# Taking the power -1/2 of every norm on VectorE instead of GpSimd in a two-layer hybrid decoder trunk

## The chip, the core and the metric

One core of a Trainium2 chip runs the whole kernel. The metric is the time of one execution in microseconds, from the first to the last work of the core. Engines are named as in the profile: PE is TensorE, DVE is VectorE, ACT is ScalarE, POOL is GpSimd, SP is the SyncE whose queue issues the weight loads.

## The reference

256 tokens of width 1024 pass through two layers. In each layer, with `mod` from a small product of the condition vector with `w_ada`:

```python
h = rms_norm(x) * (1 + sc1) + sh1
proj = h @ w_in[l]                       # q, k, v, qi, ki, wi, cu
q, k = rope(rms_norm(q per head)), rope(rms_norm(k per head))
ki = rope(layer_norm(ki))
attn = attention over the 64 keys that the index scores of qi, ki, wi select
conv = silu(layer_norm(causal depthwise conv, 31 taps, of glu(cu)))
mixed = concat(rms_norm(attn, g1), rms_norm(conv, g2))
x = x + gate1 * (mixed @ w_out[l])
h2 = rms_norm(x) * (1 + sc2) + sh2
x = x + gate2 * peer_ffn(h2)             # 8 heads x 16 experts of 16384 per token
```

Every `rms_norm` and `layer_norm` needs `(mean square or variance + 1e-6) ** -0.5`, one value per token (per token and head for q and k).

## The kernel before

The program is written engine by engine, and each engine runs its instructions in the order written; semaphores tie the engines together. Tokens lie on the 128 partitions in two tiles, `t = 0` and `t = 1`. A layer has two halves.

The first half is projections, convolution, attention and the output projection. VectorE has most of it: the conv taps (`tap`, lines 1074 to 1079), the index key's norm (1151 to 1158), the head norms of q and k (1169 to 1178) with `rotate` (1069 to 1072), the index scores (1102, 1105), the selection of keys (1114, 1116), the layer norm of the convolution (1188 to 1198), its rms norm (1207), and then, interleaved, the logits of six score blocks (`logits(n)`, 1218 to 1220) and `mix(t)`, `add_branch(t)`, `second_norm(t)`. The order at the end is written out by hand:

```python
for n in range(4):
    logits(n)
mix(0)
logits(4)
logits(5)
add_branch(0)
mix(1)
second_norm(0)
add_branch(1)
second_norm(1)
```

One of the four channel groups of the convolution is done by GpSimd: 31 taps, each after the first a TENSOR_SCALAR (line 569) and a TENSOR_TENSOR (line 570). VectorE does one group as a chain in which each tap waits for the one before, and then two groups as a pair (`conv_pair`), alternating, so that a tap need only wait for the one before the last.

PE works through one list of jobs (`plan`); each job takes the next of four PSUM banks in a ring and needs that the job four places earlier has been read out. Weight blocks of 2 MB go through three slots of SBUF (`wring`); SP issues the load of block n when the last job of block n-3 is done. In layer 0 the condition's blocks (`ada`) are worked in between: blocks (0,4) to (0,9) lie between the attention's score blocks. Before `out_tile(0)`, the output projection of the first token tile, PE waits in `use_block` for both halves of `w_out`, then for `mixed_ready` from `mix(0)` on VectorE, then transposes `hb` (line 667, jobs `mT`) and multiplies (line 644).

The second half is the expert part: scores, top 16, and then 256 gathers per token tile of 512 KB each by GpSimd, which VectorE (line 1381) and PE (line 844) consume. Nothing of the change is in it.

The power is taken on GpSimd. VectorE writes the statistic to `rs`, counts up `rsqrt_asked` and waits for `rsqrt_done`; GpSimd's own `rsqrt(width)` waits for the request and runs one TENSOR_TENSOR with the operation pow (line 527). There are nine such calls in a layer: width 2 in `modulated`, for the index key, for the convolution's layer norm and for its rms norm; width 32 for the heads; width 1 in `mix(0)`, `mix(1)`, `second_norm(0)`, `second_norm(1)`. GpSimd's calls stand at fixed places of its order: two of them inside its conv taps, after taps 19 and 24 (`POOL_TAPS`); the one of `mix(0)` stands behind `mod_rows(l, 6, 9)`, a wait for stored condition rows, and behind the issue of the two `modb` transfers.

Of the kernel before, what the change touches and what calls it, by code (L numbers as in the profile page):

```python
# [25 lines left out]
I32 = mybir.dt.int32  # L26
# [5 lines left out]
P = 128  # L32
# [3 lines left out]
NEG = -1.0e30  # L36
TAKEN = -3.0e38
RING = 4
WSLOTS = 3
# [139 lines left out]
def trunk(nc, x, c, positions, w_ada, b_ada, w_in, q_norm_g, k_norm_g, idx_k_ln_g, idx_k_ln_b,  # L179
# [36 lines left out]
    with ExitStack() as ctx:  # L216
        def sb(name, shape, dt=F32):
            return ctx.enter_context(nc.sbuf_tensor(name, shape, dt))

        def sem(name):  # L220
            return ctx.enter_context(nc.semaphore(name))
# [30 lines left out]
        rs = sb("rs", [P, 32])  # L252
        neghalf = sb("neghalf", [P, 32])
        bn6 = sb("bn6", [P, 2, 6])
# [88 lines left out]
        mod2_landed = sem("mod2_landed")  # L343
        rsqrt_asked = sem("rsqrt_asked")
        rsqrt_done = sem("rsqrt_done")
        rope_ready = sem("rope_ready")
# [152 lines left out]
        def _(pool):  # L499
# [9 lines left out]
                                    base=0, pattern=[[-1, P]], channel_multiplier=1))  # L509
            seq_(pool.memset(neghalf[:, :], -0.5))  # L510
            inv_freq = np.power(np.float32(ROPE_THETA), -np.arange(0, ROT, 2, dtype=np.float32) / ROT)
            for i, f in enumerate(inv_freq):
                seq_(pool.memset(invf[:, i:i + 1], float(f)))
            for i, first in enumerate(cand_start):
# [4 lines left out]
                           allow_slow_non_contiguous=True).then_inc(pos_landed, 16)  # L519

            asked = 0

            def rsqrt(width):
                nonlocal asked
                asked += 1
                pool.wait_ge(rsqrt_asked, asked)
                pool.tensor_tensor(rs[:, 0:width], rs[:, 0:width], neghalf[:, 0:width],  # L527
                                   ALU.pow).then_inc(rsqrt_done, 1)

# [9 lines left out]
            for l in range(L):  # L539
# [12 lines left out]
                for i in range(2):  # L552
                    spread(moda[:, i, :], scratch[l, i * D:(i + 1) * D].partition_broadcast(P), mod1_landed)
                rsqrt(2)
                pool.wait_ge(h_ready, 2 * (l + 1))
# [11 lines left out]
                for i in range(1, TAPS):  # L567
                    p = tap_tmp[:, i % 2, 0:T]
                    seq_(pool.tensor_scalar(p, hc[:, ct, i:i + T], cwT[:, ct, i:i + 1], None, ALU.mult))  # L569
                    seq_(pool.tensor_tensor(o, o, p, ALU.add), conv_pool if i == TAPS - 1 else None)  # L570
                    if i == POOL_TAPS[0]:
                        rsqrt(2)
                    if i == POOL_TAPS[1]:
                        rsqrt(32)
                rsqrt(2)
                rsqrt(2)
                mod_rows(l, 4, 5)
# [5 lines left out]
                for i in range(2):  # L583
                    spread(modb[:, i, :], scratch[l, (3 + i) * D:(4 + i) * D].partition_broadcast(P), mod2_landed)
                for t in range(2):
                    rsqrt(1)
                for t in range(2):
                    rsqrt(1)

# [413 lines left out]
        def _(dve):  # L1003
            seq_ = Chain(dve, dve_step)
            asked = [0]

            def rsqrt(last):

                seq_(last, rsqrt_asked, wait=False)
                asked[0] += 1  # L1010
                dve.wait_ge(rsqrt_done, asked[0])

# [32 lines left out]
            def rms_stats(src, t, width, junk=None):  # L1045

                return dve.tensor_tensor_reduce(out=hb[:, t, 0:width] if junk is None else junk, in0=src, in1=src,
                                                scale=1.0 / width, scalar=NORM_EPS, op0=ALU.mult, op1=ALU.add,
                                                accum_out=rs[:, t:t + 1])

            def modulated(l, mod, ready, landed):

                seq_(rms_stats(xs[:, 0, :], 0, D))
                rsqrt(rms_stats(xs[:, 1, :], 1, D))
                dve.wait_ge(landed, 32 * (l + 1))
                seq_(ts(mod[:, 1, :], mod[:, 1, :], 1.0, None, ALU.add))
                for t in range(2):
                    seq_(stt(hb[:, t, :], xs[:, t, :], rs[:, t:t + 1], mod[:, 1, :], ALU.mult, ALU.mult))
                    seq_(tt(hb[:, t, :], hb[:, t, :], mod[:, 0, :], ALU.add), ready)
# [67 lines left out]
            for l in range(L):  # L1127
# [25 lines left out]
                rsqrt(ts(rs[:, 0:2], mv[:, :, 1], NORM_EPS, None, ALU.add))  # L1153
                for t in range(2):
# [12 lines left out]
                for t in range(2):  # L1167
                    sq = hb[:, t, :].rearrange("p (h d) -> p h d", d=DH)
                    seq_(tt(sq, pjh[:, t, 0:16, :], pjh[:, t, 0:16, :], ALU.mult))
                    seq_(dve.tensor_reduce(rs[:, 16 * t:16 * t + 16], sq, AX.X, ALU.add))  # L1170
                rsqrt(ts(rs[:, 0:32], rs[:, 0:32], 1.0 / DH, NORM_EPS, ALU.mult, ALU.add))
                for t in range(2):
# [17 lines left out]
                rsqrt(ts(rs[:, 0:2], mv[:, :, 1], NORM_EPS, None, ALU.add))  # L1190
                dve.wait_ge(out_gains_landed, 64 * (l + 1))
# [7 lines left out]
                for t in range(2):  # L1199
                    dve.wait_ge(silu_done, 2 * l + t + 1)  # L1200
                    ins = rms_stats(hb[:, t, AW:D], t, CW)
                    if t:
                        rsqrt(ins)
                    else:
                        seq_(ins)
# [24 lines left out]
                def mix(t):  # L1230

                    attended(t)
                    rsqrt(dve.tensor_tensor_reduce(out=xtmp[:, 0, :], in0=hb[:, t, 0:AW], in1=hb[:, t, 0:AW],  # L1233
                                                   scale=1.0 / AW, scalar=NORM_EPS, op0=ALU.mult, op1=ALU.add,
                                                   accum_out=rs[:, 0:1]))
                    seq_(stt(hb[:, t, 0:AW], hb[:, t, 0:AW], rs[:, 0:1], out_g[:, 0:AW], ALU.mult, ALU.mult),
                         mixed_ready)
# [12 lines left out]
                def second_norm(t):  # L1250

                    if t == 0:
                        dve.wait_ge(mod2_landed, 32 * (l + 1))
                        seq_(ts(modb[:, 1, :], modb[:, 1, :], 1.0, None, ALU.add))
                    rsqrt(dve.tensor_tensor_reduce(out=hb[:, t, :], in0=xs[:, t, :], in1=xs[:, t, :],
                                                   scale=1.0 / D, scalar=NORM_EPS, op0=ALU.mult, op1=ALU.add,
                                                   accum_out=rs[:, 0:1]))
                    seq_(stt(hb[:, t, :], xs[:, t, :], rs[:, 0:1], modb[:, 1, :], ALU.mult, ALU.mult))
                    seq_(tt(hb[:, t, :], hb[:, t, :], modb[:, 0, :], ALU.add), h2_ready)
# [138 lines left out]

POOL_TAPS = (19, 24)

# [25 lines left out]
```

## Time and profile before

| | |
|---|---|
| median of 3 runs | 2205.45 us (2203.77 to 2205.62) |
| the profiled execution | 2211.21 us, span 2209.4 us |
| PE busy | 923.3 us (42%) |
| DVE busy | 1102.6 us (50%), 2632 instructions |
| ACT busy | 121.1 us (5%) |
| POOL busy | 1129.9 us (51%), 1234 instructions |
| PE clock, mean | 0.682 of full speed |

No engine is busy for more than about half of the span. The core goes through stages with different limits, so each stage has to be read by itself. The busy shares in 40 slices show the two layers: slices 1 to 7 and 21 to 26 (of 55 us each) are the compute stages, and in all others the DMA engines are near fully busy with the gathers.

### The profile page before, as it was taken

To read this page: it belongs to the slowest core of one execution; us is meant where nothing else is said; L and a number is where in the kernel's file an instruction comes from. 1 tells how busy PE (TensorE), PEld (TensorE's weight loads), DVE (VectorE), ACT (ScalarE), POOL (GpSimd) and SP (SyncE) were. 2 spreads that over 40 slices of the span, in tenths; PEclk is the share of its full clock that TensorE was granted. 3 is DMA by queue.
4 is the path that set the end of the run, shared out by engine and by line. 5 is a ranking of instruction groups with operands and counts; after the bars stand their busy time and mean duration, and the time that the engine had idled before them with its cause. 6 is when DMAs were issued, how large, how long until landed. Compare 5 with 4: busy or idle time off the path is not lost. (4 is left out here: it accounts for less than half of the span.)

```text
span 2209.4 us, 16237 instructions
## 1 busy us (share of the span) xinstructions
PE 923.3 (42%) x5604; PEld 462.6 (21%) x5604; DVE 1102.6 (50%) x2632; ACT 121.1 (5%) x255; POOL 1129.9 (51%) x1234
## 2 busy tenths in 40 slices
PE   3985898100145400035449868800014551001554
PEld 2744486100011100001117445700000110000110
DVE  1585316688752078830015852498876206884000
ACT  0122101000000000000001121100000000000000
POOL 1650000566667666666646500046666767666664
PEclk8987898555575755567769968955557685555677
DMA  8336268999999999999973303149999999999997
GB/s 308 120 133 230 88 236 326 409 398 370 351 359 353 356 373 377 368 357 355 368 264 108 127 29 124 39 187 385 367 379 338 350 363 382 368 370 358 373 361 303
DMA packets 208467, 652.32 MB, mean 295 GB/s; under 512 B 20201, under 2 KB 28489, under 8 KB 208385
## 3 DMA queue, kind: packets, MB, share of 16 engines
q0 software_dynamic: 150240, 545.72, 65.7%
q1 hardware_dynamic: 57952, 105.50, 13.2%
q8 instruction: 45, 0.74, 0.1%
q14 instruction: 38, 0.30, 0.0%
q10 hardware_dynamic: 192, 0.05, 0.0%
HBM read 650.11 MB, written 1.10 MB: 295 GB/s over the span
## 5 line engine op out<-in xcount | busy, mean ns | idle before, releaser
L602 POOL DMA_INDIRECT rows<-in_peer_u,u_at x512 | 481.7, 941 | 415.0 <-DVE u_at L1346 174.8
L1381 DVE CUSTOM_DVE_ANT_0 rows<-rows,ps 128x1024 f32<-128x1024 f32 x512 | 603.3, 1219 | 80.3 <-issue 76.6
L610 POOL DMA_INDIRECT rows<-in_peer_v,v_at x512 | 491.7, 960 | 259.8 <-issue 128.6
L844 PE MATMUL ps<-rows,arena 128*32 128x512 f32 x2048 | 385.3, 891 | 345.1 <-DMA rows<-in_peer_v,v_at 299.8
L644 PE MATMUL ps<-arena 128*128 128x256 f32 (+2 forms) x1216 | 355.1, 455 | 10.3 <-ACTq L887 6.2
L667 PE MATMUL ps<-ident,coef 128*128 128x128 f32 x4 | 1.9, 476 | 747.5 <-DVE coef L1387 377.3
L644 PEld LDWEIGHTS ps<-arena 128*128 128x128 f32 x1216 | 233.3, 197 | 127.9 <-issue 92.6
L844 PEld LDWEIGHTS ps<-rows,arena 128*32 128x32 f32 x2048 | 80.0, 140 | 645.2 <-issue 643.9
L1364 DVE TENSOR_TENSOR bias<-ps,arena 128x512 f32<-128x512 f32 x8 | 5.5, 690 | 356.2 <-PE ps L844 356.1
L667 PEld LDWEIGHTS ps<-ident,coef 128*128 128x128 f32 x4 | 0.7, 182 | 748.6 <-DVE coef L1387 377.8
L527 POOL TENSOR_TENSOR rs<-rs,neghalf 128x2 f32<-128x2 f32 (+2 forms) x18 | 21.1, 1175 | 213.3 <-DVE rs L1233 73.8
L1349 DVE CAST v_at<-ps 128x128 uint32<-128x128 f32 x4 | 1.2, 291 | 240.9 <-remote 240.5
L1079 DVE SCALAR_TENSOR_TENSOR arena<-arena,cwT 128x256 f32<-128x256 f32 x180 | 90.0, 550 | 2.4
L667 PE MATMUL ps<-ident,arena 128*128 128x128 f32 (+1 forms) x252 | 48.7, 354 | 89.3 <-ACTq L953 25.3
L884 ACT COPY arena<-ps 128x512 f32<-128x512 f32 (+2 forms) x110 | 62.5, 569 | 357.4 <-PE ps L644 214.4
L659 PE MATMUL ps<-arena,cact 128*32 128x128 f32 x1536 | 62.8, 330 | 45.7 <-DMA brows<-in_b_ada 32.7
L1274 DVE MAX8 arena<-arena 128x8 f32<-128x128 f32 x64 | 15.6, 286 | 132.7 <-ACTq L887 116.6
L659 PEld LDWEIGHTS ps<-arena,cact 128*32 128x32 f32 x1536 | 53.3, 134 | 53.8 <-issue 27.9
L569 POOL TENSOR_SCALAR arena<-arena,cwT 128x256 f32<-128x256 f32 x60 | 61.0, 1017 | 5.5
L537 POOL DMA_DIRECT2D arena<-mod_rows x12 | 6.7, 567 | 107.6 <-DMA mod_rows<-stages 104.7
L667 PEld LDWEIGHTS ps<-ident,arena 128*128 128x128 f32 (+1 forms) x252 | 38.9, 186 | 100.4 <-issue 30.5
L997 ACT ACTIVATE dots<-dots 128x128 f32<-128x128 f32 x4 | 1.2, 309 | 995.0 <-remote 796.0
(161 smaller groups left out, 723.7 us busy)
## 6 DMA issues: line engine op xcount, KB each, us to landing
arena<-in_w_ada SPq DMA_DIRECT2D x24, 2048.0 KB
arena<-in_w_in SPq DMA_DIRECT2D x8, 2048.0 KB
arena<-in_peer_wq SPq DMA_DIRECT2D x8, 2048.0 KB
arena<-in_w_in SPq DMA_DIRECT2D x8, 1024.0 KB
arena<-in_w_out SPq DMA_DIRECT2D x4, 2048.0 KB
rows<-in_peer_u,u_at POOLq DMA_INDIRECT x512
rows<-in_peer_v,v_at POOLq DMA_INDIRECT x512
arena<-mod_rows POOLq DMA_DIRECT2D x12, 512.0 KB, 5.5
```

What stands on the lines that cost most here:

```text
L527: pool.tensor_tensor(rs[:, 0:width], rs[:, 0:width], neghalf[:, 0:width], ALU.pow).then_inc(rsqrt_done, 1)
L569: seq_(pool.tensor_scalar(p, hc[:, ct, i:i + T], cwT[:, ct, i:i + 1], None, ALU.mult))
L602: pool.indirect_dma_start(row(n), None, u_rows, bass.IndirectOffsetOnAxis(ap=u_at[:, t, k:k + 1], axis=0)).then_inc(row_landed[n % SLOTS], 16)
L610: pool.indirect_dma_start(row(n), None, v_rows, bass.IndirectOffsetOnAxis(ap=v_at[:, t, tok:tok + 1], axis=0)).then_inc(row_landed[n % SLO ...
L644: ins = pe.matmul(o, a, b, start=i == 0, stop=i == len(pairs) - 1)
L659: ins = pe.matmul(o[32 * q:32 * q + 32, 0:P], lhs, rhs, start=k == 0, stop=k == KT)
L667: ins = pe.transpose(o[:, i * n:(i + 1) * n], s, ident[0:n, 0:n])
L844: ins = pe.matmul(ps[32 * g:32 * g + 32, YB + q, :], spread_c[:, g, a, :], row(n)[:, q * 512:q * 512 + 512], start=a == 0, stop=a == 31)
L884: ins = act.copy(dst, s) if scale is None else act.mul(dst, s, scale)
L1079: return stt(o, hc[:, ct, i:i + T], cwT[:, ct, i:i + 1], o, ALU.mult, ALU.add)
L1274: seq_.lag(dve.max(v[:, 0:8], s))
L1381: dve.tensor_tensor_reduce(out=row(n), in0=row(n), in1=h2_shown, scale=1.0, scalar=0.0, op0=ALU.mult, op1=ALU.add, accum_out=dots[:, t, k: ...
```

## The change

The statistic is now formed with half its scale in a new tile `halfv`, and VectorE takes the power itself. The waits between VectorE and GpSimd for it, GpSimd's calls, the tile `neghalf` and the constant `POOL_TAPS` go away, so GpSimd's 31 taps follow each other without the two calls in between.

```diff
+SEED = float(0x5F3759DF - 2 ** 22 - 2 ** 31)
...
-            def rsqrt(width):
-                nonlocal asked
-                asked += 1
-                pool.wait_ge(rsqrt_asked, asked)
-                pool.tensor_tensor(rs[:, 0:width], rs[:, 0:width], neghalf[:, 0:width],
-                                   ALU.pow).then_inc(rsqrt_done, 1)
...
                     seq_(pool.tensor_tensor(o, o, p, ALU.add), conv_pool if i == TAPS - 1 else None)
-                    if i == POOL_TAPS[0]:
-                        rsqrt(2)
-                    if i == POOL_TAPS[1]:
-                        rsqrt(32)
-                rsqrt(2)
-                rsqrt(2)
                 mod_rows(l, 4, 5)
...
-                for t in range(2):
-                    rsqrt(1)
-                for t in range(2):
-                    rsqrt(1)
...
-            def rsqrt(last):
-
-                seq_(last, rsqrt_asked, wait=False)
-                asked[0] += 1
-                dve.wait_ge(rsqrt_done, asked[0])
+            def rsqrt(last, width):
+                seq_(last)
+                v, y, t = halfv[:, 0:width], rs[:, 0:width], newt[:, 0:width]
+                seq_(ts(y.bitcast(I32), v.bitcast(I32), -0.5, SEED, ALU.mult, ALU.add))
+                for _ in range(3):
+                    if width == 1:
+                        seq_(stt(t, y, v, y, ALU.mult, ALU.mult))
+                    else:
+                        seq_(tt(t, y, y, ALU.mult))
+                        seq_(tt(t, t, v, ALU.mult))
+                    seq_(stt(y, t, 1.5, y, ALU.subtract, ALU.mult))
...
-                                                scale=1.0 / width, scalar=NORM_EPS, op0=ALU.mult, op1=ALU.add,
-                                                accum_out=rs[:, t:t + 1])
+                                                scale=0.5 / width, scalar=0.5 * NORM_EPS, op0=ALU.mult, op1=ALU.add,
+                                                accum_out=halfv[:, t:t + 1])
```

A call of width 1 is 7 small VectorE instructions, one of width 2 or 32 is 10; each waits for the one before. The statistics keep their number of instructions (the two layer norms' TENSOR_SCALAR gets a second operation).

## Rows read from the trace of the kernel before

**Rows 1.** Groups by line on VectorE: busy, mean ns, idle before, releaser.
```profile
L1236 DVE SCALAR_TENSOR_TENSOR arena<-arena,rs 128x512 f32<-128x512 f32 x4 | 3.0, 751 | 14.9 <-POOL rs L527 14.9
...
L1175 DVE TENSOR_TENSOR arena<-arena,rs 128x1024 f32<-128x1024 f32 x4 | 5.4, 1346 | 11.3 <-POOL rs L527 11.3
...
L1155 DVE TENSOR_SCALAR arena<-arena,mv,rs 128x64 f32<-128x64 f32 x4 | 1.8, 450 | 1.9 <-POOL rs L527 1.8
```

**Rows 2.** The same view: small instructions, and one with a pointer scalar.
```profile
L1153 DVE TENSOR_SCALAR rs<-mv 128x2 f32<-128x2 f32 x2 | 0.3, 169 | 0.1
...
L1302 DVE TENSOR_TENSOR cand<-arena 128x8 f32<-128x8 f32 x32 | 4.2, 166 | 0.0
...
L1040 DVE SCALAR_TENSOR_TENSOR rope<-ropek,rope 128x32 f32<-128x32 f32 x3 | 0.6, 191 | 0.1
...
L1029 DVE TENSOR_SCALAR rope<-invf,posf 128x8 f32<-128x8 f32 x4 | 0.9, 231 | 0.1
```

**Rows 3.** Timeline of VectorE around mix(0), layer 0: start, duration, what, idle before.
```profile
203.99 0.17 DVE L1220 TENSOR_SCALAR negm<-gmx 128x2 f32<-128x2 f32 x1
204.19 0.20 DVE L1225 RECIPROCAL rinv<-rsum 128x8 f32<-128x8 f32 x1
...
218.77 0.75 DVE L1236 SCALAR_TENSOR_TENSOR arena<-arena,rs 128x512 f32<-128x512 f32 x1 [12.92 <-POOL rs L527]
```

**Rows 4.** Timeline of VectorE in layer 1, first norm.
```profile
1155.35 0.69 DVE L1056 TENSOR_SCALAR arena<-arena 128x1024 f32<-128x1024 f32 x1 [4.25 <-DMA arena<-mod_rows]
```

**Rows 5.** Timeline of GpSimd's conv taps, layer 0.
```profile
101.34 0.97 POOL L569 TENSOR_SCALAR arena<-arena,cwT 128x256 f32<-128x256 f32 x1
...
103.22 0.98 POOL L569 TENSOR_SCALAR arena<-arena,cwT 128x256 f32<-128x256 f32 x1
...
126.91 0.74 POOL L527 TENSOR_TENSOR rs<-rs,neghalf 128x2 f32<-128x2 f32 x1 [21.90 <-DVE rs L1153]
```

**Rows 6.** Line 1079 in two windows: ns min/median/max, first and last start.
```profile
L1079 DVE SCALAR_TENSOR_TENSOR arena<-arena,cwT x7: 473/695/946, 100.2 to 103.9; 128x256 f32<-128x256 f32 x7
...
L1079 DVE SCALAR_TENSOR_TENSOR arena<-arena,cwT x40: 472/478/483, 109.6 to 125.1; 128x256 f32<-128x256 f32 x40
```

**Rows 7.** Groups by line on VectorE, after GpSimd's taps resume.
```profile
L1105 DVE SCALAR_TENSOR_TENSOR arena<-arena,wis 128x128 f32<-128x128 f32 x14 | 7.2, 518 | 0.5
...
L1072 DVE TENSOR_TENSOR arena<-arena 128x72 f32<-128x72 f32 x4 | 2.6, 641 | 0.1
...
L1158 DVE TENSOR_TENSOR arena<-arena,gain_small 128x128 f32<-128x128 f32 x2 | 1.4, 698 | 0.1
...
L1071 DVE TENSOR_TENSOR arena<-arena 128x72 f32<-128x72 f32 x4 | 0.9, 232 | 0.1
...
L1102 DVE TENSOR_SCALAR arena<-arena,wis 128x128 f32<-128x128 f32 x2 | 0.7, 352 | 0.1
...
L1157 DVE TENSOR_TENSOR arena<-arena,gain_small 128x128 f32<-128x128 f32 x2 | 0.6, 293 | 0.1
```

**Rows 8.** Timeline of PE at the output projection of both token tiles, layer 0.
```profile
220.39 1.08 PE L667 MATMUL ps<-ident,arena 128*128 128x128 f32 x4 [8.31 <-DVE arena L1218]
...
223.78 1.22 PE L644 MATMUL ps<-arena 128*128 128x512 f32 x1 [0.72 <-ACTq L887]
...
249.50 1.97 PE L667 MATMUL ps<-ident,arena 128*128 128x128 f32 x8 [3.25 <-DVE arena L1236]
252.19 10.29 PE L644 MATMUL ps<-arena 128*128 128x512 f32 x19 [0.72 <-ACTq L887]
```

**Rows 9.** SP's queue: the issue of the two w_out loads, layer 0.
```profile
200.86 5.30 SPq L485 DMA_DIRECT2D arena<-in_w_out  x2
```

**Rows 10.** Windows: us, busy of PE, PEld, DVE, ACT, POOL, clock, DMA share, GB/s.
```profile
198.00:216.80 18.80, 14.08 (x272) 10.94 (x264) 3.14 (x7) 5.01 (x15) 0.00 (x0) 0.95 0.99 362
308.65:315.85 7.20, 6.42 (x160) 5.43 (x160) 0.90 (x6) 2.29 (x5) 0.00 (x0) 1.00 0.88 290
```

**Rows 11.** Timeline of PE: the first matmul of a wq block loaded from 308.65 on.
```profile
317.83 1.22 PE L644 MATMUL ps<-arena 128*128 128x256 f32 x2 [2.76 <-DMA arena<-in_peer_wq]
```

More of the change, by code:

```diff
@@ L252, in trunk @@
         rs = sb("rs", [P, 32])
-        neghalf = sb("neghalf", [P, 32])
+        halfv = sb("halfv", [P, 32])
+        newt = sb("newt", [P, 32])
         bn6 = sb("bn6", [P, 2, 6])
@@ L343, in trunk @@
         mod2_landed = sem("mod2_landed")
-        rsqrt_asked = sem("rsqrt_asked")
-        rsqrt_done = sem("rsqrt_done")
         rope_ready = sem("rope_ready")
@@ L509, in _ @@
                                     base=0, pattern=[[-1, P]], channel_multiplier=1))
-            seq_(pool.memset(neghalf[:, :], -0.5))
             inv_freq = np.power(np.float32(ROPE_THETA), -np.arange(0, ROT, 2, dtype=np.float32) / ROT)
@@ L519, in _ @@
                            allow_slow_non_contiguous=True).then_inc(pos_landed, 16)
-            asked = 0
-            def rsqrt(width):
-                nonlocal asked
-                asked += 1
-                pool.wait_ge(rsqrt_asked, asked)
-                pool.tensor_tensor(rs[:, 0:width], rs[:, 0:width], neghalf[:, 0:width],
-                                   ALU.pow).then_inc(rsqrt_done, 1)
             def mod_rows(l, first, last):
@@ L570, in _ @@
                     seq_(pool.tensor_tensor(o, o, p, ALU.add), conv_pool if i == TAPS - 1 else None)
-                    if i == POOL_TAPS[0]:
-                        rsqrt(2)
-                    if i == POOL_TAPS[1]:
-                        rsqrt(32)
-                rsqrt(2)
-                rsqrt(2)
                 mod_rows(l, 4, 5)
@@ L1004, in _ @@
             seq_ = Chain(dve, dve_step)
-            asked = [0]
-            def rsqrt(last):
-                seq_(last, rsqrt_asked, wait=False)
-                asked[0] += 1
-                dve.wait_ge(rsqrt_done, asked[0])
+            def rsqrt(last, width):
[9 more added lines that the diff above has]
+                    seq_(stt(y, t, 1.5, y, ALU.subtract, ALU.mult))
             def take(name):
@@ L1047, in rms_stats @@
                 return dve.tensor_tensor_reduce(out=hb[:, t, 0:width] if junk is None else junk, in0=src, in1=src,
-                                                scale=1.0 / width, scalar=NORM_EPS, op0=ALU.mult, op1=ALU.add,
-                                                accum_out=rs[:, t:t + 1])
+                                                scale=0.5 / width, scalar=0.5 * NORM_EPS, op0=ALU.mult, op1=ALU.add,
+                                                accum_out=halfv[:, t:t + 1])
             def modulated(l, mod, ready, landed):
                 seq_(rms_stats(xs[:, 0, :], 0, D))
-                rsqrt(rms_stats(xs[:, 1, :], 1, D))
+                rsqrt(rms_stats(xs[:, 1, :], 1, D), 2)
                 dve.wait_ge(landed, 32 * (l + 1))
@@ L1152, in _ @@
                     seq_(dve.bn_aggr(mv[:, t, :], bn6[:, t, :]))
-                rsqrt(ts(rs[:, 0:2], mv[:, :, 1], NORM_EPS, None, ALU.add))
+                rsqrt(ts(halfv[:, 0:2], mv[:, :, 1], 0.5, 0.5 * NORM_EPS, ALU.mult, ALU.add), 2)
                 for t in range(2):
@@ L1169, in _ @@
                     seq_(tt(sq, pjh[:, t, 0:16, :], pjh[:, t, 0:16, :], ALU.mult))
-                    seq_(dve.tensor_reduce(rs[:, 16 * t:16 * t + 16], sq, AX.X, ALU.add))
-                rsqrt(ts(rs[:, 0:32], rs[:, 0:32], 1.0 / DH, NORM_EPS, ALU.mult, ALU.add))
+                    seq_(dve.tensor_reduce(halfv[:, 16 * t:16 * t + 16], sq, AX.X, ALU.add))
+                rsqrt(ts(halfv[:, 0:32], halfv[:, 0:32], 0.5 / DH, 0.5 * NORM_EPS, ALU.mult, ALU.add), 32)
                 for t in range(2):
@@ L1189, in _ @@
                     seq_(dve.bn_aggr(mv[:, t, :], bn6[:, t, :]))
-                rsqrt(ts(rs[:, 0:2], mv[:, :, 1], NORM_EPS, None, ALU.add))
+                rsqrt(ts(halfv[:, 0:2], mv[:, :, 1], 0.5, 0.5 * NORM_EPS, ALU.mult, ALU.add), 2)
                 dve.wait_ge(out_gains_landed, 64 * (l + 1))
@@ L1202, in _ @@
                     if t:
-                        rsqrt(ins)
+                        rsqrt(ins, 2)
                     else:
@@ L1233, in mix @@
                     rsqrt(dve.tensor_tensor_reduce(out=xtmp[:, 0, :], in0=hb[:, t, 0:AW], in1=hb[:, t, 0:AW],
-                                                   scale=1.0 / AW, scalar=NORM_EPS, op0=ALU.mult, op1=ALU.add,
-                                                   accum_out=rs[:, 0:1]))
+                                                   scale=0.5 / AW, scalar=0.5 * NORM_EPS, op0=ALU.mult, op1=ALU.add,
+                                                   accum_out=halfv[:, 0:1]), 1)
                     seq_(stt(hb[:, t, 0:AW], hb[:, t, 0:AW], rs[:, 0:1], out_g[:, 0:AW], ALU.mult, ALU.mult),
@@ L1255, in second_norm @@
                     rsqrt(dve.tensor_tensor_reduce(out=hb[:, t, :], in0=xs[:, t, :], in1=xs[:, t, :],
-                                                   scale=1.0 / D, scalar=NORM_EPS, op0=ALU.mult, op1=ALU.add,
-                                                   accum_out=rs[:, 0:1]))
+                                                   scale=0.5 / D, scalar=0.5 * NORM_EPS, op0=ALU.mult, op1=ALU.add,
+                                                   accum_out=halfv[:, 0:1]), 1)
                     seq_(stt(hb[:, t, :], xs[:, t, :], rs[:, 0:1], modb[:, 1, :], ALU.mult, ALU.mult))
@@ L1397 @@
 CONV_ORDER = (2, 3, 0, 1)
-POOL_TAPS = (19, 24)
 DOTS = [(0, (0, 2, 4, 6), 128), (0, (1, 3, 5, 7), 128),
```

## The prediction

> **What bounds the kernel now.** I read the page first, then the groups by line on VectorE, then the timelines of DVE, POOL and PE through each layer's first half. The page shows no engine above about half of the span, so only stages count. All nine calls of a layer lie in its first half; the expert half, which is most of the time, contains none and follows whatever the first half does, because its gathers start from addresses that come last. From the end of the conv projections to the first score block VectorE runs without a pause, except where it waits for the power; what it loses or wins there moves everything behind it. After that PE and VectorE take turns.
>
> The reader should see two sizes of wait [rows 1]. Line 1175, the head norms, stood 11.3 us before two instructions, 5.6 each. Line 1155 stood 0.9 each time. Line 1236 stood 14.9 over four, but 12.9 of it is one case, `mix(0)` of layer 0 [rows 3]; the other three are 0.7 each. So the power itself is dear only at width 32, and the long wait is not the power but GpSimd's order: the call stands behind a wait for stored rows.
>
> **The price of a call on VectorE.** Small instructions take 0.166 to 0.191 us, and one with a pointer scalar 0.231 against about 0.17 [rows 2]; between two that depend on each other lie about 0.03 us (203.99 + 0.17 to 204.19) [rows 3]. Ten instructions of width 2 make 10 x 0.20 = 2.0; ten of width 32 make 10 x 0.22 = 2.2; seven of width 1, three with a pointer scalar, make 4 x 0.20 + 3 x 0.26 = 1.6. No row has a bit-cast integer operand; I bound it by the smallest and largest small rows, 0.17 and 0.23, which is 0.06 per call, and take 0.17.
>
> **The change part by part, for one layer.**
> 1. First norm (`modulated`). VectorE then waits 4.25 us for the `mod_rows` transfer in layer 1 [rows 4] and far longer in layer 0. The longer call costs 1.2 and is covered: 0. Without that cover it would be 1.2.
> 2. Index key: 2.0 for a wait of 0.9: +1.1.
> 3. Heads: 2.2 for 5.6: -3.4.
> 4. Conv layer norm and conv rms norm: like 2, +1.1 each.
> 5. `mix(1)`: 1.6 for 0.7. PE waits for line 1236 there [rows 8]: +0.9, say +1.0 with the extra gap. `second_norm(1)`: PE has nothing else, +1.0. `second_norm(0)` runs while PE multiplies for the second tile (252.19, over 10 us) [rows 8]: 0. `mix(0)` of layer 1: PE still has score blocks and a transpose to do: 0, at most 1.0.
> 6. The moved work. GpSimd stopped after tap 19 and idled 21.9 us until the index key asked [rows 5]; eleven taps came only after that. Without the call they follow at once, beside VectorE's `conv_pair`. How that pair runs beside GpSimd is in the trace: GpSimd's taps are 1.88 us apart (101.34 to 103.22) [rows 5], and VectorE's start every 0.62 (six steps from 100.2 to 103.9), against 0.397 (39 steps from 109.6 to 125.1) once GpSimd is still [rows 6]. That is three VectorE taps for one of GpSimd's. Eleven taps last 11 x 1.88 = 20.7 us and cover 33 VectorE taps, each (1.88/3 - 0.397) = 0.23 dearer: +7.6.
> 7. The same eleven taps no longer stand beside what follows the index key. Line 1072 took 0.641 against 0.232 for line 1071 of the same shape, two a layer: 0.8. Line 1158 took 0.698 against 0.293: 0.4. Line 1105 took 0.518 where the same width takes 0.352 with a pointer scalar, seven a layer: 1.2 [rows 7]. These give 2.4. The other two-input lines of the stretch (the rest of `rotate`, the gains, line 1175) have had the same company. The upper bound is what the same eleven taps cost in part 6, 7.6; between 2.4 and 7.6 I take 5.3, a little above the middle, as the rows shown are less than half of the stretch's two-input instructions: -5.3.
>
> Up to the first score block that is 1.1 - 3.4 + 2.2 + 7.6 - 5.3 = +2.2 per layer (between -0.1 and +5.1 by part 7's bounds). Adding part 5, layer 1 is +4.2.
>
> A rule of the Trainium skill bears on part 6 (SBUF — State Buffer, "SBUF: two separate sides"): VectorE instructions with two SBUF inputs and GpSimd instructions take one shared port pair as an exclusive lock, held for the whole instruction. Taken strictly, the trace does not agree, as three VectorE taps get through in each 1.88 us of GpSimd's; what the strict rule would make of the sum is worked out below as a rival.
>
> **Layer 0, the 12.9 us.** Removing the wait lets `mix(0)` end about 11 us earlier. What is late next? PE's transposes started at 220.39, released by line 1218, which is behind `mix(0)` on VectorE [rows 8]. But PE also needs both halves of `w_out`, issued at 200.86 and just before 206.16 [rows 9]. From 198.0 to 216.8 the DMA engines moved 362 GB/s x 18.8 us = 6.8 MB [rows 10]: that is 0.5 MB already in flight and three blocks of 2.1 MB, an `ada` block and then the two halves of `w_out`. Another block had its 2.1 MB (290 x 7.2) at 315.85 [rows 10], and PE began on it at 317.83 [rows 11], 2.0 later. So the weights land between 216.8 and 218.8; I take 218.3. The load's issue hangs on PE's earlier jobs, so it moves by the +2.2: PE starts at 220.6, +0.2. Both transposes' banks are then free, so transposes to matmul takes 2.7 as at the second tile instead of 3.4 (249.50 to 252.19, 220.39 to 223.78) [rows 8]: -0.7. After `mix(0)` layer 0 thus stands at -0.5, and with part 5 at +1.5. The long wait is nearly worthless: the weights take its place.
>
> **Sum.** 1.5 + 4.2 = +5.7 us. The profiled execution took 2211.21 us (span 2209.4, and 1.8 around it), 0.26% above the median of the runs; it would become 2216.9, the median 2205.45 + 5.7 = 2211.2. What a measurement can tell from no change is about 0.2%, 4.4 us, so the forecast lies just beyond.
>
> **The rivals.**
> A. Sum near zero: part 7 gives back nearly all that part 6 takes (7.6), which is -2.3 per layer, or the weights are there at 216.8 (-1.5). Then +1 to +4, 2206.5 to 2209.8. For it: the same instructions of GpSimd move from one place to another. Against: VectorE's taps are nearly all two-input work and the later stretch has reduces and small instructions too. Chance 0.25.
> B. Faster: the pair of tap chains yields to nothing beside GpSimd. The slow steps of [rows 6] would then belong to the start of the pair, and part 6 costs nothing: 5.7 - 15.2 = -9.5, 2196. It decides from a part 6 below about 0.3 of my price (a sum of -4.4 needs 10.1 less, 5.0 per layer, so below 2.6). Against it: the steps become even exactly when GpSimd stops at 105. Chance 0.06.
> C. Much slower: VectorE and GpSimd exclude each other for a whole instruction. Then one VectorE tap of 0.47 [rows 6] fits behind each GpSimd instruction, two in each of its taps, which then lasts 1.88 + 2 x 0.47 = 2.8 us: eleven take 31 us with 22 VectorE taps instead of 78 (31/0.397), so 56 x 0.397 = +22 instead of +7.6 per layer: 5.7 + 29 = +35, 2240. Against: the same two streams were together from 100 to 104 without that. Chance 0.03. The Trainium skill's section named above is the rule behind this case.
> D. The wait of `mix(0)` is worth its face because the weights were long there: layer 0 wins some 6 more, sum -0.5, 2205. Against: the bytes above. Chance 0.06.
>
> **How the numbers follow.** Forecast +4.4 to +10: 0.60; A 0.25, B 0.06, C 0.03, D 0.06. The bounds of part 7 alone are +/- 5 over both layers, but both ends at once with part 6's price are unlikely. The range from 2206.5 (A's lower end) to 2216 (part 7 at 2.9 a layer) leaves out B, D and C and a little on either side. Slower by over 0.2% is the forecast and C, 0.63; within 0.2% is A, D and a little, 0.30; faster 0.07. The time is 2211.2.
>
> **What would show it.** In the profile after: no line 527; 156 more DVE instructions (4 x 7 + 5 x 10 in each layer); GpSimd's last tap of layer 0 near 126, and line 1079 slow (starts 0.62 apart) up to it; lines 1072, 1158 and 1105 at 0.23, 0.29 and 0.35; about 2.0 us from line 1153 to line 1155 and 2.2 to 2.4 between 1171 and 1175; PE's transposes before `out_tile(0)` at about 220.6, released by the `w_out` load; PE's waits for lines 1236 and 1259 longer by 1. I am wrong if the paired taps keep 0.4 us beside GpSimd, if part 7 gives back 7 or more, or if PE starts on `out_tile(0)` well before 219.

## The result, and the profile after

The changed kernel took 2220.03 us in the median of 4 runs (2218.35 to 2222.49), the kernel before 2204.61 beside it (4 runs): ratio 1.0071, 95% interval 1.0054 to 1.0089, or +15.4 us (11.9 to 19.6). Forecast were 2211.2 us, a range of 2206.5 to 2216.0 and a sum of +5.7. The side was right; the cost is 2.7 times the sum, and the time lies outside the range.

The profiled execution after has a span of 2216.6 us, with 156 more DVE instructions, as forecast. First the groups by line on VectorE that answer to [rows 1], [rows 2] and [rows 7]; the lines stand some 16 lower in the new file (1236 is now 1220, 1175 is 1159, 1155 is 1139, 1072 is 1056, 1105 is 1089, 1158 is 1142).

```profile
L991 DVE SCALAR_TENSOR_TENSOR newt<-rs,halfv 128x1 f32<-128x1 f32 x24 | 5.3, 219 | 0.9
...
L994 DVE TENSOR_TENSOR newt<-newt,halfv 128x2 f32<-128x2 f32 (+1 forms) x30 | 5.0, 167 | 1.0
...
L1159 DVE TENSOR_TENSOR arena<-arena,rs 128x1024 f32<-128x1024 f32 x4 | 4.9, 1226 | 0.1
...
L1220 DVE SCALAR_TENSOR_TENSOR arena<-arena,rs 128x512 f32<-128x512 f32 x4 | 3.0, 751 | 0.1
...
L1139 DVE TENSOR_SCALAR arena<-arena,mv,rs 128x64 f32<-128x64 f32 x4 | 1.3, 314 | 0.1
```

The 28 us of waiting of [rows 1] are gone: the last field of lines 1159, 1220 and 1139 is 0.1. With the shapes kept apart, the lines of [rows 7] now run alone:

```profile
L1089 DVE SCALAR_TENSOR_TENSOR arena<-arena,wis 128x128 f32<-128x128 f32 x14 | 4.9, 352 | 0.5
...
L1056 DVE TENSOR_TENSOR arena<-arena 128x72 f32<-128x72 f32 x4 | 0.9, 233 | 0.1
...
L1142 DVE TENSOR_TENSOR arena<-arena,gain_small 128x128 f32<-128x128 f32 x2 | 0.6, 292 | 0.1
```

The conv taps of layer 0, VectorE's in two windows and the last of GpSimd's timeline (against [rows 5] and [rows 6]):

```profile
L1063 DVE SCALAR_TENSOR_TENSOR arena<-arena,cwT x42: 471/695/948, 102.1 to 127.5; 128x256 f32<-128x256 f32 x42
...
L1063 DVE SCALAR_TENSOR_TENSOR arena<-arena,cwT x19: 472/473/946, 127.5 to 135.2; 128x256 f32<-128x256 f32 x19
```

```profile
124.47 0.97 POOL L558 TENSOR_SCALAR arena<-arena,cwT 128x256 f32<-128x256 f32 x1
...
126.35 0.97 POOL L558 TENSOR_SCALAR arena<-arena,cwT 128x256 f32<-128x256 f32 x1
```

GpSimd no longer stops; its taps start 1.88 us apart and VectorE's 0.62 apart (25.4 us for 41 steps) until it ends at 128.1. Parts 6 and 7 were read rightly.

Now `mix(0)` of layer 0 on VectorE, and PE around `out_tile(0)` (against [rows 3] and [rows 8]):

```profile
210.97 0.15 DVE L988 TENSOR_SCALAR rs<-halfv 128x1 int32<-128x1 int32 x1
211.16 0.22 DVE L991 SCALAR_TENSOR_TENSOR newt<-rs,halfv 128x1 f32<-128x1 f32 x1
211.42 0.16 DVE L995 SCALAR_TENSOR_TENSOR rs<-newt,rs 128x1 f32<-128x1 f32 x1
...
212.51 0.75 DVE L1220 SCALAR_TENSOR_TENSOR arena<-arena,rs 128x512 f32<-128x512 f32 x1
```

```profile
224.59 1.94 PE L646 MATMUL ps<-ident,arena 128*128 128x128 f32 x8 [7.43 <-issue]
227.25 16.00 PE L623 MATMUL ps<-arena 128*128 128x512 f32 x32 [0.72 <-ACTq L866]
...
253.83 1.97 PE L646 MATMUL ps<-ident,arena 128*128 128x128 f32 x8 [4.14 <-DVE arena L1220]
```

The wait of 12.92 us is gone and `mix(0)` ends 6.3 us earlier, yet PE starts 4.2 later than in [rows 8]. It waited for nothing of VectorE's.

The view of the tile `in_w_out` puts these 7.4 us of waiting down to the load of `w_out`. Its issue came at 205.94, 5.1 us later than in [rows 9].

The next view was none of those the prediction named: windows of the DMA engines in stretches that load weights (the last field is GB/s, the one before it the engines' busy share). Before:

```profile
24.00:38.00 14.00, 8.55 (x178) 6.10 (x168) 0.00 (x0) 1.06 (x4) 0.00 (x0) 0.98 1.07 389
380.00:400.00 20.00, 12.21 (x276) 9.89 (x276) 13.06 (x13) 0.80 (x3) 4.86 (x5) 0.83 1.06 404
```

and after:

```profile
24.00:38.00 14.00, 8.85 (x192) 6.57 (x181) 0.00 (x0) 1.06 (x4) 0.00 (x0) 0.79 1.07 363
...
380.00:400.00 20.00, 13.12 (x252) 10.38 (x256) 19.07 (x68) 0.80 (x3) 0.00 (x0) 0.62 1.05 388
```

The engines are as busy and move 7% and 4% less. In the second window gathers have begun before, at 393.8; cut off at 393 the two rates are 406 and 390. In the first window VectorE does nothing in either kernel, and the first norm is applied only behind it. A change of some VectorE and GpSimd instructions has made DMA slower. At the end of layer 0's routing PE waits for such blocks. Its timeline after, each row the start on a block of `ada` weights, every second block shown:

```profile
387.22 2.65 PE L638 MATMUL ps<-arena,cact 128*32 128x128 f32 x64 [1.61 <-DMA brows<-in_b_ada]
...
398.10 3.64 PE L638 MATMUL ps<-arena,cact 128*32 128x128 f32 x64 [1.21 <-DMA brows<-in_b_ada]
...
409.09 2.77 PE L638 MATMUL ps<-arena,cact 128*32 128x128 f32 x44 [3.11 <-DMA brows<-in_b_ada]
```

That is 10.9 us for two blocks, and before:

```profile
375.67 3.49 PE L659 MATMUL ps<-arena,cact 128*32 128x128 f32 x64 [1.46 <-DMA brows<-in_b_ada]
...
385.60 3.62 PE L659 MATMUL ps<-arena,cact 128*32 128x128 f32 x64 [2.82 <-DMA brows<-in_b_ada]
...
395.88 3.22 PE L659 MATMUL ps<-arena,cact 128*32 128x128 f32 x56 [2.81 <-DMA brows<-in_b_ada]
```

10.1. These waits are the smaller part of what the routing loses. Of the 6.05 us lost between the first top-k instruction and v's addresses (table below), 5.2 stand already at the `ada` block that PE starts at 355.20 before and at 366.47 after. 3.1 of them are two products with `peer_wq`, which took 17.03 and 15.73 us for 15.54 and 14.08, at a granted clock of 0.82 and 0.89 for 0.90 and 1.00; the other 2.1 are waits ahead of them.

How much later the same instruction starts after than before, in us, from both timelines:

```
                                  layer 0   layer 1
first norm applied                 +2.21     +5.95
last conv tap                     +10.07    +13.65
first score block (logits(0))      +4.38     +7.98
score block behind mix(0)          -6.26     +8.86
second_norm(1)                     +6.09     +9.88
first top-k instruction            +6.07    +11.67
v's row addresses, first tile     +12.12    +11.66
```

From the first conv tap (+2.43, +6.00) to the first score block the loss is 1.95 and 1.98, where the prediction had 2.2. What it has not is the +2.2 ahead of everything, the +6 at the end of layer 0's routing, and part of what lies between `mix(0)` and `second_norm(1)`.

### The profile page after: what moved, and what is told of

It is laid out like the page before. It is cut to its first block and busy times, and to the rows that moved or that the text cites. A ratio compares the mean times of both kernels' runs of the same rounds, so it can differ in the third digit from the quotient of the medians.

```text
span 2216.6 us, 16368 instructions
## 1 busy us (share of the span) xinstructions
PE 928.1 (42%) x5604; PEld 466.0 (21%) x5604; DVE 1136.1 (51%) x2788; ACT 121.2 (5%) x255; POOL 1102.1 (50%) x1215
## 5 line engine op out<-in xcount | busy, mean ns | idle before, releaser
L623 PE MATMUL ps<-arena 128*128 128x256 f32 (+2 forms) x1216 | 360.5, 460 | 11.9 <-DMA arena<-in_peer_wq 6.2
L1063 DVE SCALAR_TENSOR_TENSOR arena<-arena,cwT 128x256 f32<-128x256 f32 x180 | 105.2, 634 | 2.4
L559 POOL TENSOR_TENSOR arena<-arena 128x256 f32<-128x256 f32 x60 | 45.9, 764 | 5.0
```

The source lines that it names most:

```text
L623: ins = pe.matmul(o, a, b, start=i == 0, stop=i == len(pairs) - 1)
L1063: return stt(o, hc[:, ct, i:i + T], cwT[:, ct, i:i + 1], o, ALU.mult, ALU.add)
```

## The experiments

Four groups; within a group all kernels ran beside the same kernel before.

**First group: the two halves of the change.** e1 is the kernel before and e2 the changed kernel, on another chip. e3 has all powers on VectorE, but GpSimd's taps stop where they stopped before:

```
# e3, GpSimd, in the loop over its taps; VectorE raises taps_go behind
# the conv taps and again behind the head statistics
 if i == POOL_TAPS[0]:
-    rsqrt(2)
+    pool.wait_ge(taps_go, 2 * l + 1)
 if i == POOL_TAPS[1]:
-    rsqrt(32)
+    pool.wait_ge(taps_go, 2 * l + 2)
# e4: all powers stay GpSimd's, the two calls move behind its last tap
-    if i == POOL_TAPS[0]: rsqrt(2)
-    if i == POOL_TAPS[1]: rsqrt(32)
+rsqrt(2)
+rsqrt(32)
```

> The kernel before once more, with a trace on the same chip as the next three runs. All theories: within 0.2% of the other runs of it. In the two traces at hand line 1056 starts 2.2 us later after the change although nothing of the change lies ahead of it, and the DMA engines move 387 GB/s where they moved 406; if that is the execution and not the change, this trace has a value of its own for both.

> The changed kernel once more, for a paired time and trace. +15 us over before (the first measurement said 1.0054 to 1.0089). My sum said +5.7; the trace shows its terms up to the first score block nearly as priced (+2.0 per layer), so the rest must lie behind: in PE's slower clock after longer pauses, and in the weight loads of layer 0 that are late.

> The changed kernel, but GpSimd's taps stop again after tap 19 until VectorE has ended its conv taps, and after tap 24 until the head statistics are there; all powers stay on VectorE. Theory 1 (the moved taps cost what parts 6 and 7 say, +7.6 - 5.6 = +2.0 per layer): 4 us less than the changed kernel, still some 11 over before. Rival (the moved taps are the loss and all Newton steps are cheap): 12 or more less than the changed kernel. Rival (the Newton instructions alone cost it): no change from it.

> The kernel before with all powers on GpSimd, only that GpSimd's calls for the index key and the heads stand behind the last tap, so that the taps follow each other as in the changed kernel. Theory 1: +2.0 us per layer, +4 over before (0.2%). Rival that the moved taps are the loss: +12 or more.

Measured: before 2074.03 us on this chip (14 runs; e1 is one more, 2078.07), e2 2090.44, ratio 1.0074 (1.0056 to 1.0091); e3 1.0028 (1.0017 to 1.0038), +6.0 us; e4 1.0034 (1.0022 to 1.0046), +7.6 us. Expected were +11 for e3 and +4 for e4, and both lie outside their intervals; the next groups show why. In e4's trace the last conv tap falls 7.61 us further back than the first, and 1.74 is left at the first score block; in e2's 7.62 and 1.97. So part 6 is a cost of the taps' new place alone. e3's trace surprised too: without that cost it should have come to about -0.1 per layer by the first score block, and it has +0.94 and +0.96. The index key's power there took 3.5 us from line 1188 to line 1192 instead of 2.0:

```profile
126.58 0.17 DVE L1188 TENSOR_SCALAR halfv<-mv 128x2 f32<-128x2 f32 x1
126.79 0.68 DVE L1036 TENSOR_SCALAR rs<-halfv 128x2 int32<-128x2 int32 x1
...
128.65 0.64 DVE L1043 SCALAR_TENSOR_TENSOR rs<-newt,rs 128x2 f32<-128x2 f32 x1
...
129.52 0.34 DVE L1042 TENSOR_TENSOR newt<-newt,halfv 128x2 f32<-128x2 f32 x1
...
130.09 1.07 DVE L1192 TENSOR_SCALAR arena<-arena,mv,rs 128x64 f32<-128x64 f32 x2
```

GpSimd's taps start again at 125.71 there, and instructions of 0.16 us take up to 0.68 beside them. So in these traces a power on VectorE has its price of 2.0 us only while GpSimd is still. One thing set e2 apart from both halves: from 380 to 400 us its DMA engines moved 387 GB/s, those of e3 and e4 403 and 407. Both kept `neghalf` beside the new tiles, so their tiles lay elsewhere than the changed kernel's. That gave the theory for the next group.

**Second group: where the tiles lie, and the heads alone.** The change removes one tile of 128 bytes per partition (`neghalf`) and adds two (`halfv`, `newt`), all declared ahead of `arena`, which holds the weights. By the compiled program's list of addresses `arena` starts at 97024 before, a multiple of 256, and 128 later after. e5 is the kernel before, and e6 the changed kernel, with one more unused tile:

```
# e5                                    # e6
 neghalf = sb("neghalf", [P, 32])        newt = sb("newt", [P, 32])
+pad = sb("pad", [P, 32])               +pad = sb("pad", [P, 32])
# e7 and e8: the changed kernel's power only where listed, GpSimd's elsewhere
+ON_DVE = [(0, 'qk'), (1, 'qk')]                 # e7: heads, both layers
+ON_DVE = [(0, 'mix0'), (0, 'qk'), (1, 'qk')]    # e8: and mix(0), layer 0
```

> The kernel before, with one unused tile of 128 bytes per partition declared ahead of the tiles that hold the weights, so that every tile behind it lies 128 bytes further on, as in the changed kernel. No instruction differs. Theory L (the shifted tiles make the weight loads slower): in the window 380 to 400 us the DMA engines move about 387 GB/s instead of about 402, in all weight-bound stretches likewise, and the run is 4 to 9 us above the kernel before. Rival N (the lower rate in the changed kernel is a result of its other timing, not of addresses): 402 GB/s and within 2 us of the kernel before.

> The changed kernel with a further unused tile of 128 bytes, which puts the weights' tiles a whole 256 bytes behind their place in the kernel before. No instruction differs from the changed kernel. Theory L: the weight loads are back at some 402 GB/s and the run is 4 to 9 us faster than the changed kernel, so 6 to 11 us above the kernel before. Rival N: as the changed kernel, 15 to 17 us above the kernel before.

> Only the width-32 power of the head norms is taken on VectorE; all other powers stay GpSimd's and its taps stop where they did before. The weights' tiles lie 256 bytes behind their place before. By the term of the prediction: -3.4 us in each layer, in sum about -7 us if nothing behind eats it, the first score block of each layer 3.4 earlier. Rival: what comes behind (the weights for out_tile in layer 0) eats layer 0's part, in sum -3 to -4 us.

> As the one before it, and the power of mix(0) in layer 0 on VectorE too, so that the 12.9 us wait behind the stored rows is gone. By the prediction the weights take the wait's place: a further gain of 1 to 3 us at most against the run before it (PE starts on out_tile(0) when w_out has landed). Rival D: the wait is worth its face value, a further gain of 6 us or more.

Measured beside 24 runs of before (2204.36 us): e5 2210.64, ratio 1.0025 (1.0012 to 1.0039); e6 2213.07, 1.0038 (1.0021 to 1.0055), +8.7 us; e7 2195.78, 0.9963 (0.9950 to 0.9976); e8 2193.19, 0.9955 (0.9939 to 0.9971). Windows of e5, no instruction of which differs from before:

```profile
24.00:38.00 14.00, 8.78 (x188) 6.57 (x176) 0.00 (x0) 0.81 (x4) 0.00 (x0) 0.74 1.07 364
380.00:400.00 20.00, 13.99 (x264) 10.46 (x256) 19.14 (x51) 1.06 (x4) 0.00 (x0) 0.59 1.05 386
```

and of e6:

```profile
24.00:38.00 14.00, 7.13 (x160) 5.38 (x156) 0.00 (x0) 1.06 (x4) 0.00 (x0) 0.74 1.07 389
380.00:400.00 20.00, 14.04 (x301) 10.79 (x294) 15.82 (x16) 1.06 (x4) 2.77 (x3) 0.74 1.05 403
```

An unused tile alone takes the rate from 404 to 386 GB/s and costs 6 us; another gives the changed kernel its rate back and 6.7 of its 15.4 us. Theory L holds, rival N falls. In e5's trace the pieces look like the changed kernel's: +3.00 at the first norm, and +10.75 at v's addresses for the first tile. But there only +0.91 of it is left at the second tile's, and e7, whose tiles are even and whose rate is 403, also loses 5.0 between top-k and v's addresses, with the same two slow products (17.09 and 15.77 us). So how much of that piece belongs to the loads is open; the 6 us rest on the times.

e7: -8.6 us for 2 x 3.4 = 6.8 forecast, most of it in the trace by the first score block: 3.65 a layer from the first tap (-0.69 to -4.34). That this is so near 3.4 is partly luck. GpSimd's taps stop only after the 19th in e7 and e8; the stop after the 24th went away with the call, against what e7's expectation says. They run beside the heads' power, which takes 3.4 us (138.55 to 141.95), so 2.0 are won there, and 1.6 behind it, since the last tap starts at 149.16 instead of 156.60. e8 gains 2.6 us more, within the intervals of nothing. Its `mix(0)` starts its last instruction 10.7 us before e7's, the first output block is added only 1.7 earlier, and at `second_norm(1)` nothing is left (-3.98 and -4.02 against before). The weights take the wait's place, as forecast; rival D falls. PE's two rows in e8:

```profile
216.23 1.94 PE L678 MATMUL ps<-ident,arena 128*128 128x128 f32 x8 [7.22 <-issue]
218.89 11.35 PE L655 MATMUL ps<-arena 128*128 128x512 f32 x22 [0.72 <-ACTq L898]
```

**Third group: which start is the good one.** The kernel before with unused tiles of other sizes (e9 64 bytes, e10 208, e11 80), and e8 with 208 (e12):

```
# e9: 16, e10 and e12: 52, e11: 20
+pad = sb("pad", [P, 16])
```

> The kernel before with an unused tile of 64 bytes per partition ahead of the weights' tiles. Which remainder matters is open: a shift of 128 bytes cost 4% of the load rate, one of 256 nothing. If only the remainder by 128 counts, 64 is as bad as or worse than nothing and 128 would have been free, which it was not; if the remainder by 256 counts, this run lies anywhere between 388 and 404 GB/s in the stretch from 380 to 400 us. Theory L says that the time follows that rate: 404 gives the time of before, 388 gives 4 to 9 us more. Rival N: no dependence of the time on the rate.

> The kernel before with an unused tile of 208 bytes, which by the sizes of the tiles puts the weights' tiles on a multiple of 256 bytes (they lie 48 behind one before). If an even start were better than the one before had, the rate from 380 to 400 us is above 404 GB/s and the time falls by up to some us; if 48 behind is as good, nothing changes, within 2 us.

> The kernel before with an unused tile of 80 bytes: the weights' tiles start 128 bytes behind a multiple of 256, the changed kernel's 176 behind. If the upper half of 256 bytes is the bad one, 388 GB/s and 4 to 9 us more; if a start on a multiple of 64 bytes is what counts, 404 and the time of before.

> The kernel with the heads' power in both layers and mix(0)'s in layer 0 on VectorE and all else GpSimd's, with the weights' tiles moved to a multiple of 256 bytes. If the even start is worth nothing: as without it, 8 to 12 us below the kernel before. If it is worth something: more, by what the run with 208 unused bytes shows.

The expectations count the tiles' bytes; the compiled program rounds each tile up to 32 bytes, so the real starts are those below, and 208 was no even start at all.

```
          arena starts at    past a multiple   GB/s       against before
                             of 256 by         24 to 38   (95% interval)
before    97024                0               389
e6        97280                0               389        (changed kernel)
e9        97088               64               364        +0.36% (0.22 to 0.50)
e11       97120               96               365        +0.24% (0.11 to 0.37)
e5        97152              128               364        +0.25% (0.12 to 0.39)
after     97152              128               363        (changed kernel)
e10       97248              224               364        +0.26% (0.15 to 0.36)
e12       97504              224               364        -0.21% (-0.35 to -0.07)
```

Every start off a multiple of 256 bytes costs the same, 25 of 389 GB/s and 5 to 8 us, however far off it is. e12 gains 0.24% less than e8 did. The first norm is applied at 49.8 to 51.6 us in the seven traces with an uneven start of `arena` and at 47.6 to 49.4 in ten of the eleven others; e4 has 51.1.

The Trainium skill (DMA: Bandwidth & Descriptors, "How a descriptor splits into AXI transactions") says by the vendor's account that a descriptor is cut at multiples of 256 bytes, so one that starts off them needs one transaction more, and that the part of the first one before the start still costs beats. The page speaks of what a transaction reads; here the tile that is written moved. The runs agree with one more piece a packet, nine instead of eight for 2 KB, though they show only its price. They don't bear out the count in beats, by which a start 224 bytes off would cost more than one 64 off: both have 364 GB/s. I hadn't drawn on it, because I had not seen that the change moves tiles.

**Fourth group: the gathered rows, and the rest of the loss.** `rows`, into which the expert half gathers 537 MB (1024 gathers of 512 KB), starts at 24704 in every kernel so far, 128 past a multiple of 256. e13 is the kernel before and e14 the changed kernel with both tiles even, e15 is e6 once more, e16 is e8 with both even:

```
# e13, e14, e16: ahead of all tiles (e13 and e16 also a pad ahead of arena)
+lead = sb("lead", [P, 32])
 xs = sb("xs", [P, 2, D])
 rows = sb("rows", [P, SLOTS, D])
```

> The kernel before with two unused tiles of 128 bytes per partition, one ahead of all tiles and one behind neghalf. In the compiled program the gathered rows' tile, which stood 128 bytes behind a multiple of 256, and the weights' tiles, which stood on one, now both stand on one. The gathers' packets have 4 KB and took 170 to 177 ns. Theory S (a start off a multiple of 256 bytes costs a fixed 4 ns or so a packet, whatever its length): the expert half's rate rises from 349 to 370 GB/s by 2%, and as its some 1400 us are mostly transfers, the time falls by 15 to 30 us. Rival R (4 KB packets have this hidden, as twice the 85 ns of an even 2 KB packet is their 170): the expert half's rate and the time stay, within 3 us.

> The changed kernel with one unused tile of 128 bytes ahead of all tiles, so that the gathered rows' and the weights' tiles both stand on a multiple of 256 bytes. Rival R: as the changed kernel with its weights' tiles moved alone, 4 to 12 us above the kernel before. Theory S: 15 to 30 us below that.

> The changed kernel with its weights' tiles back on a multiple of 256 bytes, once more on this chip, to narrow the interval: the prediction's own sum is +5.7 us, the first measurement was +8.4 (4.6 to 12.1). If PE's lower clock behind the longer pauses adds to the sum, this comes out at 7 to 9 again; if the first measurement was high by chance, at 5 to 6.

> The heads' power in both layers and mix(0)'s of layer 0 on VectorE, all else GpSimd's, and both the gathered rows' and the weights' tiles on a multiple of 256 bytes. Rival R: 8 to 12 us below the kernel before, as with the weights' tiles alone. Theory S: 25 to 40 us below.

Measured beside 9 runs of before (2073.91): e13 2044.53, ratio 0.9857 (0.9842 to 0.9872), -29.4 us; e14 2053.55, 0.9910 (0.9895 to 0.9926); e15 2083.66, 1.0049 (1.0035 to 1.0063), +9.8 us; e16 2036.04, 0.9814 (0.9801 to 0.9827), -37.9 us. The windows of a stretch that only gathers, e1 (before on this kind of chip) and then e13:

```profile
1500.00:1540.00 40.00, 0.00 (x0) 0.00 (x0) 38.43 (x63) 0.00 (x0) 30.26 (x33) 0.50 1.03 410
```

```profile
1500.00:1540.00 40.00, 0.00 (x0) 0.00 (x0) 38.71 (x63) 0.00 (x0) 30.24 (x33) 0.50 1.03 420
```

2.4% more on 4 KB packets; theory S holds, rival R falls. `lead` moves every tile, but it is the gathers' rate that rose. The mean duration of these packets in the traces is 163 ns in e1 and 159 in e13. From 24 to 38 us the weights come in packets of 2 KB, 84.5 ns before and 88.5 after, and of 1 KB, 46.7 and 51.2. So an uneven start costs about 4 ns a packet, whether it has 1, 2 or 4 KB.

With both tiles even, the change costs 2053.55 - 2044.53 = 9.0 us, and e15 has +9.8, e6 +8.7. So +5.7 was still 3 us short; e15's interval (7.3 to 13.1) leaves it out, e6's (4.6 to 12.1) does not. The shifts between e13 and e14, net of where the first tap of the layer stands (-1.59 and +2.24):

```
                                  layer 0            layer 1
first score block (logits(0))      +1.98              +2.00
score block behind mix(0)          (weights)          +2.88
first output block added           +0.28              +3.82
third output block added           +2.40              +5.90
second_norm(1)                     +3.33              +6.81
first top-k instruction            +3.34              +6.59
```

In layer 1 the longer power of `mix(0)` puts VectorE's next score block back by 0.9 (+2.88 for +2.00), but nothing of that reaches PE. Its first output product starts 22.9 us behind the first score block in both kernels (22.75 to 22.91 in all traces). What makes the first output block late is the product itself, 1.8 us longer. PE in e13 and in e14:

```profile
1233.09 14.00 PE L646 MATMUL ps<-arena 128*128 128x512 f32 x32 [0.72 <-ACTq L889]
```

```profile
1237.32 15.83 PE L624 MATMUL ps<-arena 128*128 128x512 f32 x32 [0.72 <-ACTq L867]
```

In its first 4 us the granted clock was 1.00 in e13 and 0.53 in e14, and 1.00 behind them in both. The product took 15.8 to 16.3 us in e2, e4, e6, e14 and e15 and 14.0 in all other traces. e4 has every power on GpSimd and e3, with 14.0, every power on VectorE, so it goes with the taps that follow each other and not with the powers. It isn't in every execution: the profiled one of the changed kernel has 14.0. Why PE's clock rises later there is open.

From the first to the third output block the loss is 2.1 in both layers, where 1.0 was priced. PE's timelines of e13 and of e14 in layer 1, from the last eight matmuls of the attention on:

```profile
1251.86 1.10 PE L755 MATMUL ps<-arena 128*128 128x64 f32 x8 [0.78 <-ACTq L889]
1256.21 1.97 PE L669 MATMUL ps<-ident,arena 128*128 128x128 f32 x8 [3.24 <-DVE arena L1238]
1258.89 16.10 PE L646 MATMUL ps<-arena 128*128 128x512 f32 x32 [0.72 <-ACTq L889]
```

```profile
1257.92 1.83 PE L733 MATMUL ps<-arena 128*128 128x64 f32 x8 [0.78 <-ACTq L867]
1263.89 1.97 PE L647 MATMUL ps<-ident,arena 128*128 128x128 f32 x8 [4.14 <-DVE arena L1221]
1266.58 16.55 PE L624 MATMUL ps<-arena 128*128 128x512 f32 x32 [0.72 <-ACTq L867]
```

The wait for the mix is 0.9 longer, as priced; the last eight matmuls of the attention took 1.83 us for 1.10, and the projection 16.55 for 16.10: 0.7 and 0.45 more. The granted clock was 0.80 in the stretch around the eight (1255.2 to 1260.0) against 0.97 (1249.0 to 1253.2), and 0.85 against 0.87 in the projection's; in the wait for the mix both had 0.50, which is 1.2 GHz. So in e14 it fell while the eight still ran, in e13 only behind them. That it falls earlier because PE had waited longer before was not tested by itself. The layers' ends, 3.3 and 6.6, make 9.9, of which 9.0 are left in the time.

## Why the prediction was right and wrong

**Parts 1 to 4.** Right. The powers of width 2 cost +1.09 (index key), +1.09 (conv layer norm) and +1.18 (conv rms) net, for 1.1 each; the heads -3.43 for -3.4. The bit-cast instruction takes 0.15 us at width 1, 0.17 at 2 and 0.18 at 32, for 0.17.

**Part 6, the moved taps.** Right: +7.64 in each layer for 7.6, which e4 gives to their place alone. Rivals B (no contention) and C (an exclusive lock) fall by the same row: the three VectorE taps to one of GpSimd's hold over all 42 taps. The rule of the Trainium skill named in the prediction, taken strictly, is not borne out by this trace.

**Part 7, given back.** 5.6 a layer for 5.3 (-1.8 before the squares, -2.6 and -1.2 around the index scores). Rival A, which had part 7 give back 7.6, falls.

**Layer 0's long wait.** Right in kind: PE waits for `w_out` instead, and the removed wait was worth nothing at `second_norm(1)` (e8 against e7). PE started on `out_tile(0)` at 219.5 in e6, whose first score block stood at +0.51; the prediction's own terms give 218.3 + 0.5 = 218.8.

**Part 5.** The step that failed in a small way: it priced PE's waits and left PE's work as long as it was. "`mix(0)` of layer 1: PE still has score blocks and a transpose to do: 0, at most 1.0" was right about the wait, 0 at PE's start; but the output product behind it took 1.8 us longer at a lower granted clock. And "`mix(1)`: +1.0" counted only the wait; with PE's lower clock behind it the two output tiles cost 2.1 in each layer. Up to the first output block layer 0 has +0.3 where the prediction had -0.5. Layer 0 so came to 3.3 for 1.5 and layer 1 to 6.6 for 4.2: the measured cost at equal starts of the tiles is +9.0 (e14 against e13), in place of +5.7. That the clock fell or rose when it did follows from nothing tested here. In the two traces of the first section, where the first product takes 14.0 us in both, layer 1 comes to +3.9 from its first tap to `second_norm(1)`, near the 4.2.

**The sum.** The step that failed in a large way is the closing sum itself, which took every transfer as it was: "the load's issue hangs on PE's earlier jobs, so it moves by the +2.2", with `w_out`'s landing worked out from the rate of 362 GB/s in [rows 10] as if that rate were given. The issue moved by 5.1, not by 2.2. No part prices that three tiles ahead of `arena` change. They move it by 128 bytes off a multiple of 256, and the weight loads lose 4 to 7% of their rate. That is +6.3 us by e5 against before and 6.7 by e6 against the changed kernel. In the traces about 2 of it stand before the first norm; how much of the rest falls into layer 0's routing, and how much elsewhere, is open. 9 + 6.5 = 15.5, which is the measured +15.4.

## What to carry to other kernels

When a diff adds or removes a tile, compare where every tile behind it starts: keep each destination of large DMAs on a multiple of 256 bytes (in the compiled program's addresses, which round tiles up and may put something ahead of the first), because two unused tiles of 128 bytes were worth more here (29.4 us, on the faster kind of chip, the only one where they were tried) than the change under study. If a trace after a change shows the same DMA share with fewer GB/s in a stretch ahead of the change, look there first. Price a product on PE by the granted clock that it ran at, not by its length in one trace: the same 32 matmuls of layer 1 took 14.0 to 16.3 us. And of nine powers a layer only the wide one is shown to be worth taking from GpSimd: heads alone gave -8.6 us, and all of them at even tiles cost +9.0, since GpSimd's short calls had cost 0.7 us and had kept its taps out of VectorE's way.

## What the runs showed of the hardware

- Loads of 1 KB and 2 KB pieces into a tile that starts off a multiple of 256 bytes: 363 to 365 GB/s for 383 to 391, the same for 64, 96, 128 and 224 bytes off. Gathers of 4 KB rows: 410 for 420. About 4 ns a packet in each case.
- VectorE instructions of 0.16 us can take up to 0.68 while GpSimd runs taps (e3), so a chain of ten took 3.5 us instead of 2.0.
- The same product of 32 matmuls took 14.00 us at a granted clock of 1.00 and 15.83 where its first 4 us had 0.53 (e13, e14).
- Chips differ: the kernel before took 2204 us on some and 2074 on others. From 1450 to 2000 us, nearly all gathers, every trace of the first kind moved 353 to 370 GB/s, every one of the second 406 (415 to 416 with `rows` even).
